# Norm gain rows folded into the row scale of a hybrid decoder block, with the first weight slabs in halves

## The chip, the core and the metric

The kernel runs on one core of a Trainium2 chip. Five engines work side by side and meet through semaphores: TensorE (PE in the profile), VectorE (DVE), ScalarE (ACT), GpSimd (POOL) and SyncE (SP), which here issues every DMA. The metric is device time in microseconds (us) of one launch; lower is better.

## The reference

One decoder block over 512 tokens of width 1024, in float32. What matters here are its two RMS norms, each followed by a projection:

```python
def _rmsnorm(x, g):
    xf = x.astype(jnp.float32)
    xf = xf * lax.rsqrt(jnp.mean(xf * xf, axis=-1, keepdims=True) + EPS)
    return (xf * g.astype(jnp.float32)).astype(x.dtype)

h = _rmsnorm(x, norm_mix[l])
proj = h @ w_in[l]
... two attention branches, merged and gated ...
x = x + merged @ w_out[l]
h2 = _rmsnorm(x, norm_mlp[l])
x = x + jnp.square(jax.nn.relu(h2 @ w_ff1[l])) @ w_ff2[l]
```

Each norm multiplies a token's row by one factor (the row factor) and each of the 1024 columns by a gain (`norm_mix`, `norm_mlp`). Four shorter gains of 64 belong to the norms of the attention heads.

## The kernel before

The program is written out by hand for each engine (`@block.sync`, `gpsimd`, `scalar`, `vector`, `tensor`); each engine runs its list in order, and semaphores are the only ties. Tokens lie in four row blocks of 128 (`m` = 0 to 3), the width in eight chunks of 128. Every large product is made of three matmuls, high x high, high x low and low x high parts, where the high part is the value rounded to float32r (an ACT copy) and the low part the difference (a DVE subtraction): lines 378 to 380 and 385 to 387.

Weights come as slabs of 128 x 2048 (1 MB) into four raw buffers (`load`, line 399). ACT writes a slab's high part (`act_cut`, 340), DVE its low part (`dve_cut`, 365), into one of two cut buffers. Slabs 0 and 1 are the two halves of the depth for the first column group, KVI.

**The first norm.** SP issues x block 0, six small DMAs (both norm gains as 8 x 128, and four head gains), slab 0, x block 1, slab 1, x blocks 2 and 3, and then the rest. For each block ACT squares the rows and sums them (`norm_square`, 548), POOL makes the row factor in two small steps (`rows_rsqrt`, 479), and DVE multiplies the row by it (`norm_scale`, 787). PE turns the block in two halves of four 128 x 128 transposes into PSUM banks 4 and 5 (`norm_turn`, 1085). A half is a unit `u`, two for each block. With tokens now along the columns, the gain is one number for each partition and chunk: DVE multiplies the turned half with it out of PSUM into an SBUF buffer, `rows_t` (`norm_gain`, 791). From `rows_t` ACT makes the high part (`norm_hi`, 551) and DVE the low part (`norm_lo`, 802). The gains themselves were turned by one transpose on PE (line 1106) and copied by ACT (566) into `gain`.

DVE's order is written out at lines 815 to 824: scale of block 0; its two gain multiplies and two low parts; slab 0; scale of block 1; slab 1; then scale of block 2 ahead of the gain and low parts of block 1, scale of block 3 ahead of those of block 2, and those of block 3.

PE begins with 8 filler matmuls (`keep_warm`, 1097: a zero block, result unused), the transpose of the gains, the transposes of block 0 and 27 more fillers. Then it projects block 0 with slab 0, turns block 1, and projects with slab 1; block 1's projection waits for block 1's low parts (`nt_cut`), and so on. `norm_turn` may reuse a PSUM bank as soon as the gain multiply has read it (`nt_gained`).

**The second norm** (lines 737 to 744, 1039 to 1045, 1359 to 1380) runs the same helpers inside the output projection: for each block DVE adds the projection to x (`add_to_x`), scales, and then treats the block before it; PE turns block `m-1` behind block `m`'s projection, and block 3 behind the first part of the first feed-forward product, `ff1_part(0, 0, 256)`.

## Time and profile before

| | |
|---|---|
| Median of 3 runs | 789.45 us (788.76 to 789.53) |
| The profiled execution | 790.06 us |
| Its span, first to last instruction | 788.3 us |
| PE busy | 763.3 us, 97% of the span |
| DVE, ACT, POOL busy | 402.4, 304.9, 132.8 us |
| DMA | 70.11 MB, on average 89 GB/s |

The profile shows one execution. An engine's busy time counts its instructions; PE's are pipelined, so consecutive matmuls start closer together than each one lasts, and their start-to-start distance is what they cost. The chain that ended last is followed back from the last instruction, from each step to what released it. A "record" is one row of PE in the trace: an fp32 product shows as two. The fp32 transposes and the float32r products show as one.

### The profile page before, as it was taken

Reading aid. Unit: us, or ns where it says so; the run is one execution under the profiler, and the core shown is the slowest. Engines: PE = TensorE matmul, PEld = TensorE weight load, DVE = VectorE, ACT = ScalarE, POOL = GpSimd, SP = SyncE. Lnnn points to the kernel's source line nnn. Section 1 sums busy time; section 2 is a strip of 40 time slices with the busy share of each in tenths; the row PEclk is TensorE's granted clock in tenths of the full one; section 3 lists DMA queues with packets and bytes.
Section 4 is the critical chain, followed back from the end, with each engine's and each line's share of the span. In section 5 each row is a group of like instructions: output and inputs, shape, how many; then the busy total and the mean of one; then the engine's idle time right before and its main releaser. Section 6 shows DMA issues by size and latency. Waiting matters only on the chain.

```text
span 788.3 us, 9219 instructions
## 1 busy us (share of the span) xinstructions
PE 763.3 (97%) x3588; PEld 599.2 (76%) x3588; DVE 402.4 (51%) x599; ACT 304.9 (39%) x417; POOL 132.8 (17%) x143
## 2 busy tenths in 40 slices
PE   8999999999997999899999999999999999999998
PEld 4768778777775555588888888888888888888886
DVE  5544887688796856456556433233332233233331
ACT  4325553455554676633323442114311242123310
POOL 3104325000002454003301121002100120002100
PEclk9999999999998999999999999999999999999999
DMA  8307231401011212123090313332233313332011
GB/s 290 145 15 217 103 108 56 131 27 54 16 40 53 54 54 54 54 83 127 5 310 10 107 59 104 105 107 87 74 107 106 106 63 102 102 106 92 15 53 53
DMA packets 47842, 70.11 MB, mean 89 GB/s; under 512 B 2608, under 2 KB 27200, under 8 KB 47808
## 3 DMA queue, kind: packets, MB, share of 16 engines
q1 hardware_dynamic: 47808, 69.65, 27.4%
q8 instruction: 22, 0.36, 0.2%
q14 instruction: 12, 0.10, 0.0%
HBM read 65.19 MB, written 2.10 MB: 85 GB/s over the span
## 4 chain that ended last, share of the span: by engine, by line
PE 87%; DVE 6%; ACT 2%; issue 1%; DMA 1%; POOL 1%; SPq 1%; DVEq 0%; ACTq 0%; POOLq 0%
PE ps L385 13%; PE ps L387 13%; PE ps L386 13%; PE ps L378 13%; PE ps L380 12%; PE ps L379 12%; PE ps L1222 2%; PE ps L1258 2%; PE ps L1299 1%; DVE cut_lo L369 1%; PE ps L1204 1%; PE ps L1289 1%; DMA raw<-in_w_in_dram 1%; PE ps L1234 1%; PE ps L1218 1%
## 5 line engine op out<-in xcount | busy, mean ns | idle before, releaser
L385 PE MATMUL ps<-cut_hi,a_hi 128*128 128x512 f32 x480 | 189.2, 394 | 1.0 <-DVE a_lo L806 1.0
L387 PE MATMUL ps<-cut_hi,a_lo 128*128 128x512 f32 x480 | 187.2, 390 | 0.0
L386 PE MATMUL ps<-cut_lo,a_hi 128*128 128x512 f32 x480 | 187.0, 390 | 0.0
L378 PE MATMUL ps<-b_hi,cut_hi 128*128 128x512 f32 (+1 forms) x336 | 129.8, 386 | 0.5 <-DVE b_lo L806 0.5
L379 PE MATMUL ps<-b_lo,cut_hi 128*128 128x512 f32 (+1 forms) x336 | 129.5, 386 | 0.0
L380 PE MATMUL ps<-b_hi,cut_lo 128*128 128x512 f32 (+1 forms) x336 | 129.5, 386 | 0.0
L369 DVE TENSOR_TENSOR cut_lo<-raw,cut_hi 128x2048 fp32r<-128x2048 f32 (+1 forms) x38 | 78.9, 2079 | 58.9 <-ACT cut_hi L347 58.9
L385 PEld LDWEIGHTS ps<-cut_hi,a_hi 128*128 128x128 f32 x480 | 90.2, 188 | 19.7 <-DVE a_lo L806 1.5
L387 PEld LDWEIGHTS ps<-cut_hi,a_lo 128*128 128x128 f32 x480 | 90.1, 188 | 19.2
L386 PEld LDWEIGHTS ps<-cut_lo,a_hi 128*128 128x128 f32 x480 | 90.2, 188 | 17.5
L362 DVE TENSOR_TENSOR cut_lo<-raw,cut_hi 128x2048 fp32r<-128x2048 f32 x24 | 55.0, 2293 | 83.5 <-ACT cut_hi L356 83.5
L347 ACT ACTIVATE cut_hi<-raw 128x2048 fp32r<-128x2048 f32 (+1 forms) x38 | 65.5, 1726 | 63.2 <-PE ps L387 38.3
L540 POOL TENSOR_TENSOR a_lo<-gates,a_hi 128x512 fp32r<-128x512 f32 x32 | 41.5, 1297 | 273.2 <-ACT a_hi L751 273.2
L356 ACT ACTIVATE cut_hi<-raw 128x2048 fp32r<-128x2048 f32 x24 | 45.8, 1909 | 101.9 <-PE ps L387 101.9
L378 PEld LDWEIGHTS ps<-b_hi,cut_hi 128*128 128x128 f32 x336 | 63.4, 189 | 14.5 <-DVE b_lo L806 0.7
L380 PEld LDWEIGHTS ps<-b_hi,cut_lo 128*128 128x128 f32 x336 | 63.4, 189 | 14.0
L379 PEld LDWEIGHTS ps<-b_lo,cut_hi 128*128 128x128 f32 x336 | 63.4, 189 | 13.9
L1052 DVE SCALAR_TENSOR_TENSOR gates<-ps,gates 128x512 f32<-128x512 f32 x32 | 22.1, 692 | 84.2 <-ACT gates L749 82.6
L378 PE MATMUL ps<-a_hi,cut_hi 128*128 128x512 f32 x128 | 55.4, 433 | 3.3 <-ACT gates L665 3.3
L1030 DVE TENSOR_TENSOR gates<-ps,gates 128x512 f32<-128x512 f32 x40 | 27.6, 690 | 54.5 <-PE ps L387 54.4
L749 ACT ACTIVATE gates<-ps 128x512 f32<-128x512 f32 x32 | 19.2, 599 | 90.3 <-PE ps L380 90.3
L529 POOL TENSOR_SCALAR qo_sb<-qo_sb 128x128 f32<-128x128 f32 (+3 forms) x28 | 30.2, 1080 | 132.7 <-DVE snmax L973 132.0
(136 smaller groups left out, 897.2 us busy)
## 6 DMA issues: line engine op xcount, KB each, us to landing
raw<-in_w_ff_dram SPq DMA_DIRECT2D x32, 1024.0 KB, 5.4
raw<-in_w_in_dram SPq DMA_DIRECT2D x18, 1024.0 KB, 5.2
gates<-in_x_dram SPq DMA_DIRECT2D x8, 512.0 KB, 4.9
raw<-in_w_out_dram SPq DMA_DIRECT2D x4, 1024.0 KB, 5.0
raw<-in_w_branch_sb_dram SPq DMA_DIRECT2D x2, 1024.0 KB, 5.1
raw<-in_w_branch_sa_dram SPq DMA_DIRECT2D x4, 512.0 KB, 6.2
out_dram<-gates SPq DMA_DIRECT2D x8, 256.0 KB, 2.0
gates<-sp_hi SPq DMA_DIRECT2D x8, 128.0 KB, 2.4
```

Source lines behind the costliest of these rows:

```text
L347: cut = nc.scalar.activation(cut_slot(i, cut_hi, part, parts), raw[:, i % RAW, part * w:(part + 1) * w], ACT.Copy)
L356: nc.scalar.activation(cut_slot(i, cut_hi, 0, 1), raw[:, i % RAW, :], ACT.Copy).then_inc(hi_done, 1)
L362: nc.vector.tensor_tensor(cut_slot(i, cut_lo, 0, 1), raw[:, i % RAW, :], cut_slot(i, cut_hi, 0, 1).bitcast(F32), ALU.subtract).then_inc(lo ...
L369: cut = nc.vector.tensor_tensor(cut_slot(i, cut_lo, part, parts), raw[:, i % RAW, part * w:(part + 1) * w], cut_slot(i, cut_hi, part, part ...
L378: nc.tensor.matmul(dst, w_hi, rhs_hi, start=start, stop=False)
L379: nc.tensor.matmul(dst, w_hi, rhs_lo, start=False, stop=False)
L380: return nc.tensor.matmul(dst, w_lo, rhs_hi, start=False, stop=stop)
L385: nc.tensor.matmul(dst, l_hi, w_hi, start=start, stop=False)
L386: nc.tensor.matmul(dst, l_hi, w_lo, start=False, stop=False)
L387: return nc.tensor.matmul(dst, l_lo, w_hi, start=False, stop=stop)
L529: pool.tensor_scalar(bias, sa_bias[(n - 1) % 4][:, 0:w], 2.0 ** (sa_head(n - 1) - sa_head(n)), None, ALU.mult).then_inc(bias_done, 1)
L540: pool.tensor_tensor(a_lo[:, c, :], ff_sq[c % 2], a_hi[:, c, :].bitcast(F32), ALU.subtract).then_inc(f1_cut, 1)
```

## The change

1. **Gain with the row factor.** `norm_scale` becomes one DVE instruction, (x times row factor) times gain row, over 1024 columns. `norm_gain` and `rows_t` go; `norm_hi` and `norm_lo` read the turned half in PSUM directly, and `norm_turn` waits for the low part (`nt_cut`) before it reuses a bank.
2. **Where the gain rows come from.** `norm_mix` comes as one row of 1024; PE multiplies a row of ones with it (two fp32 matmuls of 512 columns, depth 1), which spreads it over all partitions in banks 6 and 7. It stays there until block 3 is scaled. `norm_mlp` comes by a DMA that repeats its row on all partitions, issued ahead of x block 2 of the second norm.
3. **The head gains** are loaded behind the x blocks, and turned behind block 2's projection; ACT copies and scales them after block 3's high parts.
4. **Halves.** Slabs 0 and 1 are each loaded, cut and waited for in two halves of 128 x 1024. The first block's projection runs in four quarters of 6 matmuls, each behind its own wait, and block 1 is turned behind the third quarter.
5. **Filler.** 27 matmuls become 7, and write to bank 3.

```diff
-WARM = (8, 27)
+WARM = (8, 7)
...
+            def load_half(i, hf):
+                dst = raw[:, i, :].rearrange("p (k c) -> p k c", k=4)
+                sp.dma_start(dst[:, 2 * hf:2 * hf + 2, :], rows(win, 512 * i + 256 * hf, 2, GROUPS[KVI], 512)
+                             ).then_inc(raw_in[i] if hf else half_in[i], 16)
+
+            load_half(0, 0)
+            sp.dma_start(mix_row, norm_mix).then_inc(mix_row_in, 16)
+            load_half(0, 1)
             sp.dma_start(x_tok[:, 1, :], x_d[P:2 * P, :]).then_inc(x_in[1], 16)
-            load(1)
+            load_half(1, 0)
+            load_half(1, 1)
...
                 sp.wait_ge(mg_cut, 4 * (m // 2) + 4)
+                if m == 2:
+                    sp.dma_start(mlp_gain, norm_mlp.to_broadcast([P, D])).then_inc(mlp_gain_in, 16)
...
             pool.memset(minus_half[:, :], -0.5)
+            pool.memset(one_row, 1.0).then_inc(one_row_made, 1)
...
-                act.wait_ge(nt_gained, u + 1)
+                act.wait_ge(nt_done, u + 1)
                 A(dst[:, 4 * hf:4 * hf + 4, m * P:(m + 1) * P],
-                  rows_t(u).rearrange("p (a b) -> p a b", a=4), ACT.Copy).then_inc(nt_hi, 1)
+                  bank(4 + u % 2).rearrange("p (a b) -> p a b", a=4), ACT.Copy).then_inc(nt_hi, 1)
...
-                V.tensor_scalar(dst, src, row_r[:, m:m + 1], None, ALU.mult).then_inc(row_scaled, 1)
+                V.scalar_tensor_tensor(out=dst, in0=src, scalar=row_r[:, m:m + 1], in1=g,
+                                       op0=ALU.mult, op1=ALU.mult).then_inc(row_scaled, 1)
...
+            mix_gain = ps[:, 6 * S:8 * S]
+            dve.wait_ge(mix_spread, 1)
+            norm_scale(0, x_tok[:, 0, :], x_tok[:, 0, :], mix_gain)
+            dve_half(0)
+            norm_lo(0, a_hi, a_lo)
+            dve_cut(0, 1, 2)
+            norm_lo(1, a_hi, a_lo)
+            dve_half(1)
+            norm_scale(1, x_tok[:, 1, :], x_tok[:, 1, :], mix_gain)
+            dve_cut(1, 1, 2)
             for m in range(2, TB):
-                norm_scale(m, x_tok[:, m, :], x_tok[:, m, :])
-                norm_block(m - 1, 0, a_hi, a_lo)
-            norm_block(3, 0, a_hi, a_lo)
+                norm_scale(m, x_tok[:, m, :], x_tok[:, m, :], mix_gain)
+                norm_lo(2 * m - 2, a_hi, a_lo)
+                norm_lo(2 * m - 1, a_hi, a_lo)
...
                     if u >= 2:
-                        pe.wait_ge(nt_gained, u - 1)
+                        pe.wait_ge(nt_cut, u - 1)
...
-            pe.wait_ge(gains_in, 96)
-            T.transpose(bank(7, 0, 20), gain_rows[:, :], ident[0:20, 0:20]).then_inc(gain_t, 1)
+            pe.wait_ge(one_row_made, 1)
+            pe.wait_ge(mix_row_in, 16)
+            for hf in range(2):
+                mm = T.matmul(bank(6 + hf), one_row, mix_row[:, hf * S:(hf + 1) * S], start=True, stop=True)
+            mm.then_inc(mix_spread, 1)
...
+                    if first and k == 0:
+                        pe.wait_ge(half_cut, half + 1)
+                        pe.wait_ge(nt_cut, half + 1)
+                    if first and k == 2:
+                        if half:
+                            norm_turn(1, x_tok[:, 1, :])
+                        slab_ready(half)
```

DVE's list at the start of the program, before (`cut_lo` is a slab's low part, `a_lo` that of the turned x, `gates` the buffer that holds x and `rows_t`):

```order
L789 TENSOR_SCALAR gates<-gates,row_r 128x1024
L797 TENSOR_TENSOR gates<-ps,gain 128x512 x2
L806 TENSOR_TENSOR a_lo<-gates,a_hi 128x4x128 x2
L369 TENSOR_TENSOR cut_lo<-raw,cut_hi 128x2048
L789 TENSOR_SCALAR gates<-gates,row_r 128x1024
L369 TENSOR_TENSOR cut_lo<-raw,cut_hi 128x2048
L789 TENSOR_SCALAR gates<-gates,row_r 128x1024
L797 TENSOR_TENSOR gates<-ps,gain 128x512 x2
L806 TENSOR_TENSOR a_lo<-gates,a_hi 128x4x128 x2
```

And now, up to block 1's low parts:

```order
L813 SCALAR_TENSOR_TENSOR gates<-gates,row_r,ps 128x1024 [waits row_ready,mix_spread]
L825 TENSOR_TENSOR cut_lo<-raw,cut_hi 128x1024 [waits half_hi]
L820 TENSOR_TENSOR a_lo<-ps,a_hi 128x4x128 [waits nt_hi]
L375 TENSOR_TENSOR cut_lo<-raw,cut_hi 128x1024 [waits hi_done]
L820 TENSOR_TENSOR a_lo<-ps,a_hi 128x4x128 [waits nt_hi]
L825 TENSOR_TENSOR cut_lo<-raw,cut_hi 128x1024 [waits half_hi]
L813 SCALAR_TENSOR_TENSOR gates<-gates,row_r,ps 128x1024 [waits row_ready]
L375 TENSOR_TENSOR cut_lo<-raw,cut_hi 128x1024 [waits hi_done]
L813 SCALAR_TENSOR_TENSOR gates<-gates,row_r,ps 128x1024 [waits row_ready]
L820 TENSOR_TENSOR a_lo<-ps,a_hi 128x4x128 [waits nt_hi] x2
```

The gain multiplies (L797) are gone, the slabs' low parts are cut in two and stand between block 0's steps, and the first scale has a second wait.

PE's list at the start, before:

```order
L1100 MATMUL ps<-cold_b,const_b 128x512 [waits const_cut]
L1100 MATMUL ps<-cold_b,const_b 128x512 x7
L1106 MATMUL ps<-ident,lg 128x20 [waits gains_in,ident_done]
L1093 MATMUL ps<-ident,gates 128x128 [waits row_scaled]
L1093 MATMUL ps<-ident,gates 128x128 x7
L1100 MATMUL ps<-cold_b,const_b 128x512 x27
L385 MATMUL ps<-cut_hi,a_hi 128x512 [waits lo_done,nt_cut]
```

And now:

```order
L1122 MATMUL ps<-cold_b,const_b 128x512 [waits const_cut]
L1122 MATMUL ps<-cold_b,const_b 128x512 x7
L1130 MATMUL ps<-lg,dist 128x512 [waits mix_row_in,one_row_made,ident_done]
L1130 MATMUL ps<-lg,dist 128x512
L1115 MATMUL ps<-ident,gates 128x128 [waits row_scaled]
L1115 MATMUL ps<-ident,gates 128x128 x7
L1122 MATMUL ps<-cold_b,const_b 128x512 x7
L391 MATMUL ps<-cut_hi,a_hi 128x512 [waits nt_cut,half_cut]
```

The two matmuls that spread the gain row (L1130) stand between the first fillers and the transposes of block 0, in place of the gains' transpose.

DVE's list in the second norm, before, from the last slab ahead of it (`b_lo` is the low part of the second norm's output):

```order
L369 TENSOR_TENSOR cut_lo<-raw,cut_hi 128x2048 [waits hi_done] x2
L1030 TENSOR_TENSOR gates<-ps,gates 128x512 [waits wo_done]
L789 TENSOR_SCALAR gates<-gates,row_r 128x1024 [waits row_ready]
L1030 TENSOR_TENSOR gates<-ps,gates 128x512 [waits wo_done]
L789 TENSOR_SCALAR gates<-gates,row_r 128x1024 [waits row_ready]
L797 TENSOR_TENSOR gates<-ps,gain 128x512 [waits nt_cut,nt_done] x2
L806 TENSOR_TENSOR b_lo<-gates,b_hi 128x4x128 [waits nt_hi] x2
```

And now:

```order
L375 TENSOR_TENSOR cut_lo<-raw,cut_hi 128x2048 [waits hi_done] x2
L1049 TENSOR_TENSOR gates<-ps,gates 128x512 [waits wo_done]
L813 SCALAR_TENSOR_TENSOR gates<-gates,row_r 128x1024 [waits row_ready,mlp_gain_in]
L1049 TENSOR_TENSOR gates<-ps,gates 128x512 [waits wo_done]
L813 SCALAR_TENSOR_TENSOR gates<-gates,row_r 128x1024 [waits row_ready]
L820 TENSOR_TENSOR b_lo<-ps,b_hi 128x4x128 [waits nt_hi] x2
```

Each block loses its two gain multiplies; its scale has a gain row as second tensor.

## Rows read from the trace of the kernel before

**Rows 1.** The page's section 4, the chain that ended last, by engine.

```profile
PE 87%; DVE 6%; ACT 2%; issue 1%; DMA 1%; POOL 1%; SPq 1%; DVEq 0%; ACTq 0%; POOLq 0%
```

**Rows 2.** Waits of 0 to 62 us: who waited for whom, sum, times, longest.

```profile
PE ps L385 <- DVE a_lo L806: 1.0, 1, 1.0
```

**Rows 3.** PE's timeline, 0 to 16: start, duration, line, output and inputs, count, [idle before].

```profile
3.56 3.60 PE L1100 MATMUL ps<-cold_b,const_b 128*128 128x512 bf16 x8 [3.56 <-DVE const_b L785]
...
7.31 1.97 PE L1093 MATMUL ps<-ident,gates 128*128 128x128 f32 x8
9.08 6.11 PE L1100 MATMUL ps<-cold_b,const_b 128*128 128x512 bf16 x27
14.95 0.47 PE L385 MATMUL ps<-cut_hi,a_hi 128*128 128x512 f32 x1
```

**Rows 4.** The chain that ended last, around 22: start, time on it, engine and line.

```profile
21.25 1.30 DVE a_lo L806 x2
...
23.10 0.23 PE ps L386
```

**Rows 5.** Windows: length, busy PE, PEld, DVE, ACT, POOL, clock share, DMA share, GB/s.

```profile
9.08:14.95 5.87, 5.87 (x29) 2.63 (x27) 4.43 (x5) 5.43 (x6) 1.26 (x2) 1.00 1.04 404
22.60:52.00 29.40, 29.40 (x138) 22.63 (x139) 13.89 (x27) 8.51 (x17) 4.32 (x10) 1.00 0.19 67
```

**Rows 6.** The chain near 171: the fp32 matmuls of 128 columns at line 1218.

```profile
170.83 0.44 PE ps L1218 x4
```

**Rows 7.** Timeline of DVE and PE in the first norm.

```profile
12.51 2.29 DVE L369 TENSOR_TENSOR cut_lo<-raw,cut_hi 128x2048 fp32r<-128x2048 f32 x1 [1.11 <-ACT cut_hi L347]
...
25.47 1.04 PE L1093 MATMUL ps<-ident,gates 128*128 128x128 f32 x8
...
26.11 0.69 DVE L797 TENSOR_TENSOR gates<-ps,gain 128x512 f32<-128x512 f32 x1 [1.55 <-PE ps L1093]
```

**Rows 8.** Groups by line and shape, whole span: count, busy us, mean ns, idle before.

```profile
L949 DVE SCALAR_TENSOR_TENSOR lg<-ps,lg 128x1280 f32<-128x1280 f32 x8 | 11.9, 1492 | 11.9 <-ACT lg L661 11.6
...
L369 DVE TENSOR_TENSOR cut_lo<-raw,cut_hi 128x1024 fp32r<-128x1024 f32 x8 | 9.8, 1219 | 3.0 <-ACT cut_hi L347 3.0
...
L749 ACT ACTIVATE gates<-ps 128x512 f32<-128x512 f32 x32 | 19.2, 599 | 90.3 <-PE ps L380 90.3
...
L549 ACT ACTIVATE gates<-gates 128x1024 f32<-128x1024 f32 x8 | 8.4, 1053 | 13.1 <-DVE gates L1030 11.1 <-DMA gates<-in_x_dram 2.0
L347 ACT ACTIVATE cut_hi<-raw 128x1024 fp32r<-128x1024 f32 x8 | 8.4, 1048 | 0.0
```

**Rows 9.** POOL's row factor: one instance, and both steps (ns: least/median/most).

```profile
13.60 1.25 POOL L482 TENSOR_SCALAR row_ms<-row_ss 128x1 f32<-128x1 f32 x1 [7.44 <-ACT gates L549]
...
L482 POOL TENSOR_SCALAR row_ms<-row_ss x8: 192/193/1871, 5.3 to 429.5; 128x1 f32<-128x1 f32 x8
...
L483 POOL TENSOR_TENSOR row_r<-row_ms,minus_half x8: 550/554/577, 5.6 to 429.7; 128x1 f32<-128x1 f32 x8
```

**Rows 10.** Timeline of DVE and PE in the second norm.

```profile
400.09 0.69 DVE L1030 TENSOR_TENSOR gates<-ps,gates 128x512 f32<-128x512 f32 x1 [2.03 <-PE ps L387]
...
414.56 1.09 PE L1093 MATMUL ps<-ident,gates 128*128 128x128 f32 x8 [0.97 <-DVE gates L789]
...
430.34 0.75 DVE L789 TENSOR_SCALAR gates<-gates,row_r 128x1024 f32<-128x1024 f32 x1 [2.13 <-POOL row_r L483]
...
431.84 1.16 PE L1093 MATMUL ps<-ident,gates 128*128 128x128 f32 x8 [0.62 <-DVE gates L797]
...
436.33 0.39 PE L378 MATMUL ps<-b_hi,cut_hi 128*128 128x256 f32 x1 [0.47 <-DVE b_lo L806]
```

**Rows 11.** PE's longest stop: windows (clock share third from last), and the work after it.

```profile
245.00:245.50 0.50, 0.00 (x0) 0.00 (x0) 0.47 (x3) 0.00 (x0) 0.00 (x0) 0.50 0.00 0
251.50:252.00 0.50, 0.50 (x3) 0.36 (x3) 0.47 (x5) 0.07 (x1) 0.47 (x1) 0.85 0.00 0
...
246.74 0.45 PE L1289 MATMUL ps<-ident,lg 128*128 128x128 f32 x1 [4.63 <-DVE lg L1003]
```

More of the change, by code:

```diff
@@ L108, in block_kernel @@
         dist_i = dist[:, :].bitcast(I32)
-        gain = sb("gain", [P, 20], F32)
+        gain = sb("gain", [P, 4], F32)
         w_tok = sb("w_tok", [P, TB, IXH], F32)
@@ L186, in block_kernel @@
         x2_in = [sem(f"x2_in{j}") for j in range(TB)]
+        mix_row_in = sem("mix_row_in")
+        one_row_made = sem("one_row_made")
+        mix_spread = sem("mix_spread")
+        mlp_gain_in = sem("mlp_gain_in")
         gains_in = sem("gains_in")
+        half_in = [sem(f"half_in{j}") for j in range(2)]
+        half_hi = sem("half_hi")
+        half_cut = sem("half_cut")
         kw_in = sem("kw_in")
@@ L208, in block_kernel @@
         nt_done = sem("nt_done")
-        nt_gained = sem("nt_gained")
         nt_hi = sem("nt_hi")
@@ L564, in _ @@
                 if m == 0:
-                    act.wait_ge(gain_t, 1)
-                    A(gain[:, :], bank(7, 0, 20), ACT.Copy).then_inc(gain_ready, 1)
+                    act_half(0)
                     norm_hi(0, a_hi)
                     norm_hi(1, a_hi)
-                    act_cut(0)
+                    act.wait_ge(raw_in[0], 16)
+                    act_cut(0, 1, 2)
                 elif m == 1:
-                    act_cut(1)
+                    act_half(1)
+                    act.wait_ge(raw_in[1], 16)
+                    act_cut(1, 1, 2)
                 else:
@@ L576, in _ @@
             norm_hi(7, a_hi)
-            for j in (16, 18):
+            act.wait_ge(gain_t, 1)
+            A(gain[:, :], bank(7, 0, 4), ACT.Copy).then_inc(gain_ready, 1)
+            act.wait_ge(gain_ready, 1)
+            for j in (0, 2):
                 A(gain[:, j:j + 1], gain[:, j:j + 1], ACT.Copy, scale=HD ** -0.5).then_inc(gain_ready, 1)
@@ L596, in turned @@
                 if g == KVI:
-                    A(k_sa[:, t], bank(b, 0, P), ACT.Copy, scale=gain[:, 19:20])
+                    A(k_sa[:, t], bank(b, 0, P), ACT.Copy, scale=gain[:, 3:4])
                     A(q_parts[0][:, :, t], bank(b, P, 3 * P).rearrange("p (a b) -> p a b", a=2),
@@ L1099, in keep_warm @@
                 for _ in range(n):
-                    T.matmul(bank(6), ident_b, cold_b[:, :], start=True, stop=True)
+                    T.matmul(bank(3), ident_b, cold_b[:, :], start=True, stop=True)
             pe.wait_ge(const_cut, 1)
@@ L1148, in _ @@
             keep_warm(WARM[1])
-            for m in range(TB):
+            project_part(KVI, 0, 0, first=True)
+            project_part(KVI, 1, 0, first=True).then_inc(proj_done, 1)
+            for m in range(1, TB):
                 pe.wait_ge(nt_cut, 2 * m + 2)
-                if m == 0:
-                    slab_ready(0)
                 project_part(KVI, 0, m)
-                if m == 0:
-                    norm_turn(1, x_tok[:, 1, :])
-                    slab_ready(1)
                 if m == 1:
```

63 lines of the change are left out of this document (28 added, 35 removed).

## The prediction, made before the changed kernel ran

> **What bounds the kernel now.** I read the page first: TensorE (PE) carries 87% of the chain that ended last [rows 1]. So only time in which PE stands still, or works at filler, can be won. Next, who waits: in the start PE waits once, 1.0 us, for the low part of row block 1 [rows 2]. Third, PE's own timeline [rows 3]: 3.56 us idle, 8 filler matmuls, the transposes of row block 0, 27 fillers, the first projection at 14.95. Fourth, the chain ahead of row block 1's projection, which DVE's low parts end at 22.55 [rows 4], and the stretch behind it, in which PE has no gap until 52 [rows 5]. **Whatever moves the start of block 1's projection, 22.60, moves the end; an earlier 14.95 alone moves nothing.** What the reader should see: DVE and the small steps on POOL own that chain, not the transfers.
>
> **Filler and transfers.** Twenty of 35 filler matmuls go; they filled a wait and are worth nothing by themselves. Six small DMAs ahead of the first slab go to later or out, and slabs 0 and 1 come in halves. x block 0 and slab 0 are 1.57 MB, 3.9 us at 404 GB/s [rows 5]; issued from 0.8 on they land near 6 or 7, while the steps below first want the second half at 13.0. Earlier transfers are hidden, with 6 us of cover. The head gains and the k/w columns are wanted behind four row blocks of some 24 matmuls at 0.23 [rows 4], 5.5 us each, so after 40: nothing.
>
> **When the gain row is in PSUM.** This is the new wait: DVE's first scale waits for mix_spread, which PE makes behind 8 fillers, and the chain of block 0 and then of block 1 is queued behind that scale. A filler takes 0.43 (8 last until 7.1 [rows 3]), which is 512 columns at 1.2 GHz; a memset on POOL adds 0.1, so the spread starts near 7.15. It is two fp32 matmuls of 512 columns with a depth of one row, which the trace has not. Nearest is an fp32 product of 128 columns, two records each, 4 records in 0.44 [rows 6]: 0.11 a record, so 0.44 at 512 columns, 1.76 for the spread's 4 at 2.4 GHz and 3.5 at 1.2. Which level holds? The transposes start 0.22 apart (8 from 7.31 to 9.08), twice what 128 fp32 columns take later, and the 27 fillers are done by 15, 0.22 each, which is 2.4 GHz [rows 3]. So the clock rose near 9.1, and I take the same here: 1.95 us at the low level do 56%, the rest needs 0.75, the end is 9.85 and DVE starts at **10.0**. Bounds: 9.1 (high throughout), 10.8 (low throughout). Before, PE already transposed at 7.31; this wait eats the head start that shorter steps give.
>
> **The DVE chain from 10.0.** Scale and gain in one pass over 1024 columns has no row; 0.69 at 512 columns [rows 7] and 1.492 at 1280 [rows 8] put it at 1.23, where the plain scale takes 0.75 [rows 10]. A low part takes 0.69, half a slab 1.22 on DVE and 1.05 on ACT, a high part out of PSUM 0.60, a square 1.05 [rows 8] and 0.19 for its sum. Neighbours on DVE overlap by some 0.09 (a pair of low parts lasts 1.30 [rows 4]). Then:
> - DVE: scale to 11.2. PE: transposes 11.25 to 12.15; the first four are seen 0.65 after their start (25.47, 26.11 [rows 7]), at 11.9. ACT: high parts to 13.05, second half of slab 0 to 14.05. DVE: its low part to 15.3, low part of block 0 to 15.9.
> - ACT: square of block 1 to 15.15, first half of slab 1 to 16.2. DVE: its low part to 17.4, scale of block 1 to 18.55, last half slab to 19.7.
> - PE: 7 fillers to 13.7, the quarters of block 0 to 15.1, 16.7, 18.8, transposes of block 1 to 19.7, last quarter to 21.1: in time.
>
> The gain multiplies are gone, two of 0.69 for each block, but the scale is 0.47 dearer, halves repeat a fixed part, and DVE idles from 13.2 to 14.05 for ACT. Block 2's scale stands ahead of block 1's low parts on DVE, so its row factor counts. ACT squares until 18.3. POOL's first step takes 0.19, but up to 1.87 when DVE was in a cut, as the one from 13.60 that ends with DVE's cut of 12.51 at 14.85 [rows 7, 9]; the second takes 0.55 [rows 9]. The last half slab's cut runs from 18.5 to 19.7, so I take the factor at 20.25, the scale to 21.4, two low parts to 22.65. Block 1 starts at **22.7, 0.1 later than 22.60**. Should POOL slip past the cut, it is 0.5 earlier.
>
> The Trainium skill (SBUF — State Buffer, "SBUF: two separate sides") says that DVE and GpSimd hold a shared port pair by an exclusive lock, also when a DVE instruction with two SBUF inputs meets a GpSimd one that reads SBUF. By that rule the cut locks POOL out and the new scale, with its gain in PSUM, doesn't; the row at 13.60 agrees. By it the sum has the 0.1 later, without it the 0.5 earlier.
>
> **The second norm.** The gain row comes by one more DMA of 0.5 MB, 1.3 us at 404 GB/s, ahead of x blocks 2 and 3. DVE adds block 2 at 400.09 [rows 10], some 6 us after SP issues it: hidden; the price is 1.3 if that cover were gone. The scale grows by 0.47, and PE waits for it at 414.56 [rows 10]: all behind is 0.47 later. In the last block the scale, 430.34 before, ends at 432.05. PE's transposes now wait for the low parts of block 2 (nt_cut in place of nt_gained), which DVE does behind that scale: 432.65 for the first four, 433.25 for the others, where before they started at 431.84. They end at 433.7, 24 narrow matmuls at half of 0.23 and a little end at 436.65, and the last low part (435.2) is no longer late; before, this point was 436.33 [rows 10]. **Cost 0.3 us**, bounds 0 (the last stop and its 0.47 end as before) and 0.8 (both delays add).
>
> The Trainium skill (VectorE: DVE Perf Modes, "The perf-mode tier table") speaks against the change: a one-tensor fp32 pass in SBUF runs at double rate, a two-tensor pass or one on PSUM does not. The rows agree. At the double rate the scale would stay at 0.75, and the second norm would win 0.6 instead, since the old waits of 0.62 and 0.47 would go.
>
> **Sum.** 0.1 + 0.3 = 0.4 us later. Against the profiled execution, 790.06 us (span 788.3, 1.8 around it), that is 790.5; against the median of the three runs, 789.45, it is **789.9**. 0.2% is 1.6 us, about what a measurement of this kernel can tell from no change.
>
> **Rivals.**
> First, *the early spread*: the clock rises before the spread, and POOL slips past the cut. DVE starts at 9.1 and block 1 12.05 later, at 21.15: 1.45 won, 0.3 lost, 788.3. For it: one trace shows the clock's rise once. Against: its transposes from 7.31 were slow.
> Second, *slower: the clock falls*. 27 fillers kept PE busy; now PE stands still from 9.85 to 11.25 for the new wait on DVE, and between quarters. At the low level 7 fillers take 3.0 instead of 1.5, transposes 1.8 instead of 0.9, a quarter 2.6 instead of 1.4. The trace shows this once: PE stops 4.63 us before 246.74, the granted clock is 0.50 at 245, and it rises again near 251.6, after 4.9 us of work [rows 11]. With 4.9 us low from 11.25, the quarters start at 16.2, block 1's transposes end at 21.4 and its low parts at 24.0: 1.3 more, 791.2. Low until block 1 starts: about 3 more, 792.9. It decides from the point where the quarters start later than 14.9. Against: 1.4 us of stop is nearer to the 1.0 ahead of 22.60, behind which matmuls start 0.23 apart [rows 2, 4], than to the 3 us that brought 0.50.
> Third, *more than I see*: halves let blocks overlap so well that over 1.6 us come off, 787.5. Block 1's projection would have to start before 20.7, though DVE has 10.4 us of work ahead of it; so the first scale would need to start before 10.0 and DVE never idle.
> Fourth, *nothing reaches PE*: block 1 starts as before and the second norm costs nothing, 789.4; it lies in the forecast's own range.
>
> **How the numbers follow.** Forecast with its bounds and the fourth (789.0 to 790.9): 0.56. Early spread, or one of its two parts (788.0 to 789.0): 0.20. Clock falls (mostly 791.0 to 792.9): 0.16. More than I see: 0.08. The range leaves out the third and the worse half of the second: 788.0 to 791.6. Faster by over 0.2% means under 787.9: 0.08. Slower by over 0.2% means over 791.0: 0.15. Within: 0.77.
>
> **What would show it.** DVE's first scale at 10.0 and 1.23 long; four records of the spread, the last shorter than the first; block 1's projection at 22 to 23; POOL's steps for block 2 drawn out to the end of the last half cut; the scale near 413.7 at 1.23, and the work behind it 0.3 to 0.5 late. I am wrong if the first scale starts before 9, if block 0's projection matmuls stand 0.43 apart, or if PE waits between 23 and 400 where it did not.

## The result, and the profile after

The changed kernel takes 792.17 us (median of 22 runs, 789.16 to 792.72), the kernel before, timed beside it, 789.13 (22 runs, 788.50 to 789.87). The ratio is 1.0027, with a 95% interval of 1.0021 to 1.0034. So the change costs 2.1 us by the ratio and 3.0 by the medians. A second set of 11 runs gave 1.0017 (1.0006 to 1.0028). The two measures differ because the times of the changed kernel fall into three groups. In the 33 runs of both sets they are 788.9 to 789.5 (6 runs), 790.2 to 790.8 (11) and 792.1 to 792.7 (16). The kernel before has two groups that lie closer together: in its 80 runs beside the experiments below, 788.3 to 789.2 (46 runs) and 789.2 to 790.2 (34). They are told apart by the mean granted clock of a run, the share of full speed that the profile records for TensorE: 0.997 or 0.998 in the first group, 0.995 or 0.996 in the second. The profiled execution of before, 790.06 at 0.995, is of the second. The forecast was 789.9, within 0.2% of before. What came is slower by 0.27% in the first set and by 0.17% in the second.

The profiled execution belongs to the last group: 792.67 us, with a span of 791.0 against 788.3. The page first: PE still carries the chain, 89% of it where it was 87% [rows 1].

```profile
span 791.0 us, 9166 instructions
...
PE 763.6 (97%) x3572; PEld 598.5 (76%) x3572; DVE 396.5 (50%) x585; ACT 303.6 (38%) x419; POOL 131.1 (17%) x144
...
PE 89%; DVE 6%; ACT 3%; issue 1%; POOL 1%; DVEq 0%; POOLq 0%; ACTq 0%
```

DVE has 5.9 us less work and ACT 1.3 less, and that brought nothing. PE's timeline in the start, the columns as in [rows 3]:

```profile
3.69 3.60 PE L1122 MATMUL ps<-cold_b,const_b 128*128 128x512 bf16 x8 [3.69 <-DVE const_b L809]
7.21 3.78 PE L1130 MATMUL ps<-lg,dist 1*128 1x512 f32 x4
12.37 1.97 PE L1115 MATMUL ps<-ident,gates 128*128 128x128 f32 x8 [1.38 <-DVE gates L813]
14.13 2.73 PE L1122 MATMUL ps<-cold_b,const_b 128*128 128x512 bf16 x7
16.51 0.58 PE L391 MATMUL ps<-cut_hi,a_hi 128*128 128x512 f32 x1
...
24.46 0.50 PE L391 MATMUL ps<-cut_hi,a_hi 128*128 128x512 f32 x1 [1.22 <-DVE a_lo L820]
```

L1130 is the spread, four records in 3.78 us. L1115 are transposes (L1093 before), L391 is the first product of each projection triple. The reader should see that everything up to about 15.9 runs at 1.2 GHz: the eight transposes take 1.76 to the next start, 0.22 each, and the seven fillers take 2.38, where they would take 3.0 at the low level and 1.5 at the high one. (The 15.9 is an estimate: 1.75 us at the low level and 0.63 at the high one make seven fillers in 2.38.) Before the change, the same engine had reached 2.4 GHz near 9.1 [rows 3]. Block 1's projection, which sets the end, starts at 24.46 instead of 22.60 [rows 4, 5]. DVE and POOL in the same stretch:

```profile
11.03 1.28 DVE L813 SCALAR_TENSOR_TENSOR gates<-gates,row_r,ps 128x1024 f32<-128x1024 f32 x1 [7.40 <-PE ps L1130]
...
20.27 1.22 DVE L375 TENSOR_TENSOR cut_lo<-raw,cut_hi 128x1024 fp32r<-128x1024 f32 x1
21.93 1.28 DVE L813 SCALAR_TENSOR_TENSOR gates<-gates,row_r,ps 128x1024 f32<-128x1024 f32 x1 [0.44 <-POOL row_r L498]
23.13 1.28 DVE L820 TENSOR_TENSOR a_lo<-ps,a_hi 128x512 fp32r<-128x512 f32 x2
```

```profile
20.24 1.65 POOL L498 TENSOR_TENSOR row_r<-row_ms,minus_half 128x1 f32<-128x1 f32 x1
```

DVE stands still for 7.40 us ahead of its first scale, for the spread. POOL's second step for block 2 takes 1.65 instead of 0.55. It ends at 21.89, 0.40 behind the end of DVE's last half cut, which ran from 20.27 to 21.49.

Two more places lose time. The transpose of the head gains (L1193) now stands between two projections on PE, and L1197 is the first product behind the four blocks (L1165 before, at 40.88):

```profile
37.07 0.39 PE L393 MATMUL ps<-cut_hi,a_lo 128*128 128x512 f32 x1
37.39 0.22 PE L1193 MATMUL ps<-ident,lg 4*128 4x4 f32 x1
37.54 0.50 PE L391 MATMUL ps<-cut_hi,a_hi 128*128 128x512 f32 x1
37.87 0.40 PE L392 MATMUL ps<-cut_lo,a_hi 128*128 128x512 f32 x1
...
43.11 0.40 PE L1197 MATMUL ps<-a_hi,sp_hi 128*40 128x512 f32 x1
```

From block 1's first product to this one (24.46 to 43.11) it is 18.65 now and was 18.28 (22.60 to 40.88). In the second norm both of PE's waits grew, from 0.97 to 1.58 and from 0.62 to 1.13 [rows 10]:

```profile
417.90 1.09 PE L1115 MATMUL ps<-ident,gates 128*128 128x128 f32 x8 [1.58 <-DVE gates L813]
...
435.71 1.16 PE L1115 MATMUL ps<-ident,gates 128*128 128x128 f32 x8 [1.13 <-DVE b_lo L820]
```

From DVE's add for block 1 (413.64, before 410.90) to its first work behind the norm (443.29, before 440.14) it is 29.65 and was 29.24. The sum of the three: 1.86 + 0.37 + 0.41 = 2.64, of the 2.7 by which the span grew. That they add up so well is in part luck, since other stretches changed too and cancel. Behind PE's long stop near 245 it is 10.94 to PE's next wait and was 10.41, for the clock is low there (see the section on the changed kernel again). From 443.29 to the end it is 347.7 and was 348.2 (from 440.14), though nothing was changed there; no run says why.

### The profile page after: what moved, and what is told of

The parts are those of the page before. It is cut to its first block, busy times and chain, and to the rows that moved or that the text cites. A ratio compares the mean times of both kernels' runs of the same rounds, so it can differ in the third digit from the quotient of the medians.

```text
span 791.0 us, 9166 instructions
## 1 busy us (share of the span) xinstructions
PE 763.6 (97%) x3572; PEld 598.5 (76%) x3572; DVE 396.5 (50%) x585; ACT 303.6 (38%) x419; POOL 131.1 (17%) x144
## 4 chain that ended last, share of the span: by engine, by line
PE 89%; DVE 6%; ACT 3%; issue 1%; POOL 1%; DVEq 0%; POOLq 0%; ACTq 0%
PE ps L391 13%; PE ps L392 13%; PE ps L393 13%; PE ps L384 13%; PE ps L386 12%; PE ps L385 12%; PE ps L1254 2%; PE ps L1290 2%; PE ps L1331 1%; DVE cut_lo L375 1%; PE ps L1236 1%; PE ps L1321 1%; PE ps L1266 1%; PE ps L1115 1%; PE ps L1250 1%
## 5 line engine op out<-in xcount | busy, mean ns | idle before, releaser
L391 PE MATMUL ps<-cut_hi,a_hi 128*128 128x512 f32 x480 | 189.5, 395 | 1.2 <-DVE a_lo L820 1.2
L391 PEld LDWEIGHTS ps<-cut_hi,a_hi 128*128 128x128 f32 x480 | 90.1, 188 | 19.9 <-DVE a_lo L820 1.6
L375 DVE TENSOR_TENSOR cut_lo<-raw,cut_hi 128x2048 fp32r<-128x2048 f32 (+1 forms) x38 | 76.8, 2022 | 55.3 <-ACT cut_hi L353 55.3
L353 ACT ACTIVATE cut_hi<-raw 128x2048 fp32r<-128x2048 f32 (+1 forms) x38 | 63.8, 1681 | 59.4 <-PE ps L393 34.8
```

The costliest lines, as they stand in the source:

```text
L353: cut = nc.scalar.activation(cut_slot(i, cut_hi, part, parts), raw[:, i % RAW, part * w:(part + 1) * w], ACT.Copy)
L375: cut = nc.vector.tensor_tensor(cut_slot(i, cut_lo, part, parts), raw[:, i % RAW, part * w:(part + 1) * w], cut_slot(i, cut_hi, part, part ...
L391: nc.tensor.matmul(dst, l_hi, w_hi, start=start, stop=False)
```

## The experiments

Two theories stood against each other. **A**: the new wait for the spread makes the loss, since the spread runs at the low clock and DVE's whole chain is queued behind it. **B**: the halves, the order of DVE's chain and the dearer second norm make it. All kernels below ran in three batches beside the kernel before, which had medians of 788.89, 788.74 and 789.46. The ratios are each against the kernel before in the same batch; the last column is read from one trace of each kernel.

| kernel | median us | ratio (95%) | block 1 starts |
|---|---|---|---|
| spread ahead of the fillers | 791.59 | 1.0029 (1.0018 to 1.0041) | 23.65 |
| gain row by repeating DMA | 787.35 | 0.9979 (0.9970 to 0.9988) | 19.78 |
| spread with depth 128 | 789.46 | 1.0000 (0.9991 to 1.0009) | 22.36 |
| second norm as before | 790.49 | 1.0019 (1.0010 to 1.0028) | 22.50 |
| head gains turned early | 790.35 | 1.0026 (1.0017 to 1.0036) | 22.42 |
| before, with one-row fillers | 796.10 | 1.0090 (1.0076 to 1.0103) | 29.48 |
| DMA, whole slabs | 789.80 | 1.0010 (1.0001 to 1.0019) | 22.95 |
| combined: DMA, old second norm, gains early | 786.63 | 0.9969 (0.9957 to 0.9981) | 19.96 |
| changed kernel again | 790.71 | 1.0017 (1.0006 to 1.0028) | 24.45 |
| combined, low parts first | 785.55 | 0.9951 (0.9938 to 0.9964) | 19.22 |
| changed, low parts first | 789.53 | 1.0003 (0.9993 to 1.0014) | 21.58 |
| before, with the halves alone | 788.93 | 0.9989 (0.9980 to 0.9997) | 20.77 |

### The gain row without a spread

```diff
+            sp.dma_start(mlp_gain, norm_mix.to_broadcast([P, D])).then_inc(mix_row_in, 16)
...
-            sp.dma_start(mix_row, norm_mix).then_inc(mix_row_in, 16)
...
-            mix_gain = ps[:, 6 * S:8 * S]
-            dve.wait_ge(mix_spread, 1)
+            mix_gain = mlp_gain
+            dve.wait_ge(mix_row_in, 16)
...
-                mm = T.matmul(bank(6 + hf), one_row, mix_row[:, hf * S:(hf + 1) * S], start=True, stop=True)
```

> No spread: the gain row comes repeated on all partitions by one DMA of 0.5 MB behind x block 0, the scale reads it from SBUF. Theory A: the first scale starts as early as its row factor allows, near 7; transposes near 8.3; block 1's first projection about 4 us earlier than 24.46, at 20.5 to 21.5, so 3 to 4 us less than the changed kernel and 0 to 1 us less than the kernel before (the second norm's 0.45 and the head gains' 0.34 stay). Theory B: block 1 starts no earlier than 22.6, as POOL's row factors, locked out by DVE's cuts, and ACT's share of the halves own the chain; at most 1.9 us less.

It took 787.35: 1.5 us less than before. Relative to before that is 4.6 us less than the changed kernel by the medians, and 3.8 by the ratios (0.9979 against 1.0027). PE, DVE and POOL of this kernel:

```profile
7.96 1.06 PE L1114 MATMUL ps<-ident,gates 128*128 128x128 f32 x8 [0.95 <-DVE gates L812]
...
19.78 0.50 PE L391 MATMUL ps<-cut_hi,a_hi 128*128 128x512 f32 x1 [1.55 <-DVE a_lo L819]
```

```profile
6.53 1.28 DVE L812 SCALAR_TENSOR_TENSOR gates<-gates,row_r 128x1024 f32<-128x1024 f32 x1 [3.03 <-DMA gates<-in_norm_mix_dram]
...
17.25 1.28 DVE L812 SCALAR_TENSOR_TENSOR gates<-gates,row_r 128x1024 f32<-128x1024 f32 x1 [0.72 <-POOL row_r L497]
```

The first scale starts 4.5 us earlier and block 1 4.7 us earlier. Theory B's limit (no earlier than 22.6) is broken, and theory A's own figure (20.5 to 21.5) was too late. The DMA moves 0.5 MB where the row alone is 4 KB, and it is the cheaper way: it lands at 6.5, when the row factor of block 0 has just come (6.26).

### The spread's place

```diff
-            pe.wait_ge(const_cut, 1)
-            keep_warm(WARM[0])
-            pe.wait_ge(ident_done, 1)
             pe.wait_ge(one_row_made, 1)
             pe.wait_ge(mix_row_in, 16)
...
             mm.then_inc(mix_spread, 1)
+            pe.wait_ge(const_cut, 1)
+            keep_warm(WARM[0])
+            pe.wait_ge(ident_done, 1)
```

> The two spread matmuls stand ahead of the 8 fillers on PE, nothing else. Theory A (the place of the spread and the low clock level make the loss): the spread runs from 3.7 to 7.4, DVE's first scale starts near 7.5 instead of 11.03, PE's 8 fillers run behind the spread and end near 10.9 at the low level, so the transposes start near 10.9 instead of 12.37 and block 1's first projection moves from 24.46 to about 23.0: 1.5 us less than the changed kernel. Theory B (the halves, the order of DVE's chain and the dearer second norm make it): block 1's projection stays within 0.4 of 24.46, and the time within 0.5 us of the changed kernel's.

```profile
5.37 3.75 PE L1127 MATMUL ps<-lg,dist 1*128 1x512 f32 x4 [5.37 <-DMA lg<-in_norm_mix_dram]
...
12.43 1.04 PE L1115 MATMUL ps<-ident,gates 128*128 128x128 f32 x8
```

The spread did not start at 3.7, since its row lands only at 5.37. So the scale came at 9.15, the eight fillers held the transposes back until 12.43, and block 1 started at 23.65: 0.8 earlier than in the changed kernel, not 1.5. The expectation was wrong in its first number, and the time (ratio 1.0029) shows no gain. Part of the reason is what it is compared with: about half of the changed kernel's runs are in the two lower groups. Six of the seven runs here lie at 791.4 to 791.9, about 0.7 below the changed kernel's upper group, and the seventh, the traced one, at 790.56. The row teaches something else: the transposes last 1.04 and so stand at 2.4 GHz. PE had done 3.75 us of one-row matmuls, all at 1.2 GHz, and then 3.4 us of full ones.

### The spread's depth

```diff
-        one_row = dist[0:1, 0:P]
+        one_row = dist[:, 0:P]
...
+            V.memset(lg[:, 1, 0:D], 0.0).then_inc(mix_zero, 1)
...
-                mm = T.matmul(bank(6 + hf), one_row, mix_row[:, hf * S:(hf + 1) * S], start=True, stop=True)
+                mm = T.matmul(bank(6 + hf), one_row, lg[:, 1, hf * S:(hf + 1) * S], start=True, stop=True)
```

> The spread stays behind the 8 fillers but has a depth of 128 rows (127 of them zero) instead of one; DVE clears the block ahead of the DMA, which costs about 0.5 us where nothing waits. Theory A in its strong form (a matmul of one row is no work to the clock): the granted clock rises near 9.1 as before the change, the spread's later records take half of 0.93, the first scale starts at 10.0 instead of 11.03, the transposes stand 0.11 to 0.15 apart and block 0's fillers 0.22, and block 1 starts near 23.2: 1.2 us less than the changed kernel's longer executions. Weak form (only the order on PE counts) and theory B: the spread's four records stay at 0.93 each and the first scale at 11.0, time as the changed kernel's within 0.3.

```profile
7.09 2.63 PE L1133 MATMUL ps<-lg,dist 128*128 128x512 f32 x4
11.09 1.09 PE L1118 MATMUL ps<-ident,gates 128*128 128x128 f32 x8 [1.37 <-DVE gates L816]
```

The strong form of theory A came out: a spread of 2.63 instead of 3.78, the scale at 9.76 instead of 11.03 (10.0 had been expected), transposes at 2.4 GHz. Block 1 started at 22.36, 0.8 earlier than expected. The same columns on the same engine with 127 added rows of zeros give 0.27% back, the whole loss, and no run of 11 was over 789.9.

### One-row fillers in the kernel before

```diff
-                    T.matmul(bank(6), ident_b, cold_b[:, :], start=True, stop=True)
+                    T.matmul(bank(6), ident_b[0:1, :], cold_b[0:1, :], start=True, stop=True)
```

> The kernel before the change, but its 35 fillers have a depth of one row instead of 128 (same 512 columns, same place). If matmuls of one row are no work to the clock: the granted clock does not rise near 9.1, the 27 fillers stand 0.43 apart and last until about 20.7 instead of 15, block 0's first projection moves from 14.95 to about 20.7, block 1's from 22.60 to 28 or later, and the time is 5 to 7 us longer than before. If the low clock of the changed kernel's start came of its waits and its order alone: the fillers stand 0.22 apart from 9.1 as before, block 1 starts at 22.6, and the time is that of the kernel before within 0.5.

```profile
9.01 11.70 PE L1100 MATMUL ps<-cold_b,const_b 1*128 1x512 bf16 x27
20.63 0.80 PE L385 MATMUL ps<-cut_hi,a_hi 128*128 128x512 f32 x1
...
25.49 0.51 PE L387 MATMUL ps<-cut_hi,a_lo 128*128 128x512 f32 x1
25.84 1.04 PE L1093 MATMUL ps<-ident,gates 128*128 128x128 f32 x8
```

This is the plainest row of the case. PE is busy without a gap from 3.55 on, the 27 fillers stand 0.43 apart until 20.6, and 2.4 GHz comes only near 25.5, 4.9 us after block 0's projection began. Block 1 starts at 29.48. It costs 7.4 us (5 to 7 had been expected). The waits play no part here, since the instructions and their order are those of the kernel before.

### Whole slabs, and the halves alone

The first is the kernel with the repeating DMA, with slabs 0 and 1 loaded, cut and projected in one piece. The second is the kernel before with nothing but the halves and 7 fillers instead of 27 behind the transposes.

```diff
-            load_half(0, 0)
...
-            load_half(0, 1)
+            load(0)
...
-            dve_half(0)
             norm_lo(0, a_hi, a_lo)
-            dve_cut(0, 1, 2)
             norm_lo(1, a_hi, a_lo)
-            dve_half(1)
+            dve_cut(0)
```

> As the kernel with the repeating DMA (787.35, block 1 at 19.78), but slabs 0 and 1 whole as before the change: loaded, cut and projected in one piece. If the halves carry part of the gain: ACT's and DVE's cuts of slab 0 (2.1 and 2.3) delay block 1's square and scale, and block 1 starts at 20.9, 1.1 later, 788.4 in all. If they carry nothing (the gain is all from the scale with the gain in it): within 0.3 of 787.35.

> The kernel before the change with the halves alone (loads, cuts and quarters of slabs 0 and 1, and 7 fillers instead of 27); the gain is multiplied behind the transposes as before, no spread. If the halves carry the gain: block 1 starts near 20.3 instead of 22.60, and the time is 786.6 to 787.0, 2 us less than before. If halves and the gain in the scale need each other (ACT's head start is then no use): block 1 at 22 or later, within 0.6 of before.

Whole slabs cost 2.4 us, not 1.1 (by the medians and by the ratios, against the kernel with the repeating DMA). The first row below is from the kernel with whole slabs, and behind it stand two of its windows (length, busy PE, clock share, DMA share, GB/s); the last fence is from the kernel before with the halves alone.

```profile
14.88 0.47 PE L391 MATMUL ps<-cut_hi,a_hi 128*128 128x512 f32 x1 [2.33 <-DVE cut_lo L375]
```

```profile
16.00:18.00 2.00, 2.00 (x7) 0.50 1.03 361
18.00:20.00 2.00, 2.00 (x12) 0.79 1.06 388
```

```profile
20.77 0.50 PE L388 MATMUL ps<-cut_hi,a_hi 128*128 128x512 f32 x1 [1.95 <-DVE a_lo L824]
21.11 0.48 PE L389 MATMUL ps<-cut_lo,a_hi 128*128 128x512 f32 x1
21.38 0.63 PE L390 MATMUL ps<-cut_hi,a_lo 128*128 128x512 f32 x1
```

With whole slabs PE stands still for 2.33 us, and then the granted clock is 0.50 from about 15.4 to 18.8. DVE's low parts of block 1 are done at 21.9, but PE itself is late and starts block 1 at 22.95. With the halves alone block 1 starts at 20.77, 1.8 earlier than before (20.3 had been expected), but after a stop of 1.95 the granted clock is 0.50 from 21.3 to 24.7, and 1.6 us of it are lost again: from block 1's first product to the first one behind the four blocks it is 19.86 (to 40.63) and was 18.28. The median is 788.93. So the halves are worth 2.4 us where the gain is in the scale, and 0.5 (by the medians) to 0.9 (by the ratio) where it is not. That small gain is a mixture. The traced run has a mean clock of 0.996, and seven of the 12 runs, with 0.996 or less, lie at 788.8 to 789.4. The five others have 0.997 or 0.998 and lie at 787.0 to 788.0 (middle one 787.26), where before's runs of that mean clock in the same batch have a median of 788.87. No trace shows one of the five, but 0.998 leaves no room for a fall in the start beside the one near 245, so the halves alone seem to be worth 1.6 where the clock holds. The scale with the gain in it, but with whole slabs, is worth nothing: 1.0010, in which the second norm and the head gains have their 0.8 us.

### The second norm and the head gains

The second norm gets its old form back; then, apart from that, the head gains' transpose goes from behind block 2 to the wait ahead of block 1.

```diff
...
-                    norm_scale(TB + m, xn2[m % 2], xres[:, m, :], mlp_gain)
+                    plain_scale(TB + m, xn2[m % 2], xres[:, m, :])
                 if m >= 1:
+                    norm_gain(2 * (TB + m) - 2)
+                    norm_gain(2 * (TB + m) - 1)
```

> The first norm as changed, the second norm in its old form (plain scale, gain multiplies ahead of the cuts, head gains' transpose with 12 rows). Both theories: DVE's scale ahead of 417.90 is 0.75 instead of 1.28, the wait there falls from 1.58 to 0.97, the last turn's from 1.13 to 0.62. Theory A: that is worth 0.4 us of the changed kernel's loss and no more, block 1 stays at 24.46. Theory B (the second norm carries the loss through its DMA and its waits): 1.5 us or more.

```diff
+            pe.wait_ge(gains_in, 64)
+            T.transpose(bank(3, 0, 4), gain_rows[:, :], ident[0:4, 0:4]).then_inc(gain_t, 1)
             for m in range(1, TB):
...
-                if m == 2:
-                    pe.wait_ge(gains_in, 64)
-                    T.transpose(bank(7, 0, 4), gain_rows[:, :], ident[0:4, 0:4]).then_inc(gain_t, 1)
```

> The head gains' transpose stands ahead of block 1's projection, in a wait that PE has anyway (1.22 in the changed kernel), instead of between blocks 2 and 3. If the missed term is right, the stretch from block 1's first projection to the first transposes of its result loses 0.34 (18.65 to about 18.3) and the time 0.3 us; block 1's own start stays (24.46, or 22.5 where the clock rises early). Rival: the transpose costs nothing where it stood, and the time stays within 0.1; or ACT's copy of the gains, wanted now by block 3, holds PE up.

With the old second norm the waits are 0.97 and 0.62 again and the stretch of 29.65 is 29.24: 0.41. With the gains turned early the stretch of 18.65 is 18.27: 0.38. The times agree (ratios 1.0019 and 1.0026 against 1.0027), but for the second the effect is smaller than the interval, and only its trace shows it. In the kernel with the old second norm there is also less time behind the norm, 347.4 from DVE's first work there to the end, where it was 347.7 in the changed kernel; so its whole gain is not the second norm's.

Both traces show more. PE in the kernel with the gains early, then windows of it (length, busy PE, clock share, DMA share, GB/s):

```profile
6.98 1.98 PE L1130 MATMUL ps<-lg,dist 1*128 1x512 f32 x4
10.33 1.97 PE L1115 MATMUL ps<-ident,gates 128*128 128x128 f32 x8 [1.38 <-DVE gates L813]
```

```profile
9.00:11.00 2.00, 0.67 (x3) 0.77 1.04 396
11.00:13.00 2.00, 2.00 (x10) 0.50 1.04 425
13.00:15.00 2.00, 2.00 (x10) 0.87 1.12 302
```

Here the clock rose before the spread: its four records take 1.98 instead of 3.78, and the scale starts at 8.99. But the granted clock fell to 0.50 near 10.2, at the end of the stop of 1.38 behind the spread, and stayed there until about 13.5. Block 1 starts at 22.42, 2.0 earlier than in the changed kernel's trace.

### The changed kernel again

> The changed kernel once more. If its two groups of times (789.2 to 790.8, 792.1 to 792.7) are the two levels of the clock in the spread, then a trace with a span of 789.0 or less has a spread of 1.98 to 2.2, its first scale near 9.1 and block 1 near 22.5, and a trace with a span of 790.5 or more has 3.78, 11.0 and 24.5. If the groups have another cause, the span does not go with the spread's length.

The trace has a span of 790.9, a spread of 3.78, the scale at 11.02 and block 1 at 24.45. That fits, but it is the same group once more, so the short spread is shown only by kernels that differ in one place elsewhere. The mean granted clock of every run supports the reading for the middle group: it is 0.993 or 0.994 in each of its runs, as in the trace just shown with its fall (0.993), and 0.995 or 0.996 in every other run.

What sets the two lower groups apart can be something else, far behind the change. In every trace PE stands still for 4.6 us near 245, waiting for DVE, and around the end of that stop the clock falls. Here are the stop and PE's next wait in the changed kernel, and in the changed kernel with DVE's order turned (the last experiment below):

```profile
249.09 0.44 PE L1321 MATMUL ps<-ident,lg 128*128 128x128 f32 x1 [4.64 <-DVE lg L1022]
...
260.03 0.47 PE L384 MATMUL ps<-a_hi,cut_hi 128*128 128x512 f32 x1 [0.61 <-ACT gates L689]
```

```profile
246.48 0.42 PE L1321 MATMUL ps<-ident,lg 128*128 128x128 f32 x1 [4.64 <-DVE lg L1022]
...
256.25 0.47 PE L384 MATMUL ps<-a_hi,cut_hi 128*128 128x512 f32 x1 [0.62 <-ACT gates L689]
```

The stretch of 240 to 260 shows how long the fall lasts. The columns are those of [rows 5]. First the changed kernel (before and with the gains early the share is 0.83 too), then the one with DVE's order turned (with the deep spread it is 0.91 too):

```profile
240.00:260.00 20.00, 14.79 (x67) 9.73 (x63) 13.94 (x42) 8.87 (x24) 5.41 (x8) 0.83 0.15 51
```

```profile
240.00:260.00 20.00, 14.74 (x72) 9.96 (x68) 13.81 (x44) 10.74 (x33) 6.04 (x8) 0.91 0.13 34
```

A share of 0.83 is about 6.8 us at half rate, 0.91 about 3.5. What that is worth shows in the time from the end of the stop to PE's next wait: 10.9 in both traces of the changed kernel and 10.8 with the gains early, but 9.7 to 9.8 in the five traces with the short fall. That is 1.1 to 1.2 us, about what lies between the groups at 789 and 790.5 (their medians are 1.3 apart). In the other traces with the long fall, that of the kernel before among them, more of it lies inside the stop, and it is 10.1 to 10.7. The trace with DVE's order turned has both, a fall in the start (0.83 over 10 to 20) and the short one near 245, and its run has a time of 788.86 and a mean clock of 0.996, like the runs of the group at 789. So that group can have the same start as the middle one. No trace of the changed kernel itself shows it.

### The terms together, and DVE's order

```diff
-                norm_scale(m, x_tok[:, m, :], x_tok[:, m, :], mix_gain)
                 norm_lo(2 * m - 2, a_hi, a_lo)
                 norm_lo(2 * m - 1, a_hi, a_lo)
+                norm_scale(m, x_tok[:, m, :], x_tok[:, m, :], mix_gain)
```

The first kernel has the repeating DMA, the old second norm and the early head gains. The second adds the order above to it, the third puts that order into the changed kernel.

> Gain row by the repeating DMA (no spread), the second norm in its old form, and the transpose of head gains (12 rows) in the wait ahead of block 1. If the terms add: 787.35 of the kernel with the repeating DMA, less 0.45 for the second norm and 0.34 for the transpose, is 786.6, which is 2.3 us less than before. If they do not add (PE waits for something else in the second norm, or ACT's copy of the gains is late for block 3): 787.0 or more.

> The combined kernel (786.63, block 1 at 19.96), with DVE making the two low parts of block m-1 ahead of the scale of block m instead of behind it. If that scale and its wait for POOL's row factor (0.72) own the end of the chain: the low parts end near 18.4, PE's wait of 1.41 ahead of block 1 falls to about 0.1, and the time falls by 1.2 to 1.4, to 785.3. If the high parts of ACT or PE itself are as late as the scale was: under 0.3 won. Against it: block 2's transposes then wait for its scale; they are wanted 2.8 after block 1 starts, near 21.3, and the scale ends near 19.7.

> The changed kernel with only that order turned (low parts of block m-1 ahead of the scale of block m). If the dearer scale and the POOL step that is locked out by the last half cut are on the path: block 1 starts 1.0 to 1.3 earlier than in the changed kernel, at 23.2 with the long spread or at 21.3 with the short one, and the median falls by 1.0 to 1.3 us. If the path runs through PE's transposes and ACT's high parts: block 1 within 0.3 of 24.46 or 22.5.

The terms add: 786.63 came for 786.6, closer than the traces bear out, since in this kernel too the work behind the second norm takes less than in the changed one (351.2 from the end of PE's last wait in the norm, 433.72, to the end; in the kernel before it is 352.0, from 436.33). The order is worth 1.1 us more by the medians and 1.4 by the ratios: 785.55, ratio 0.9951, the best version, 3.9 us below before. Its PE and DVE:

```profile
18.97 0.23 PE L1198 MATMUL ps<-ident,lg 12*128 12x12 f32 x1
19.22 0.50 PE L396 MATMUL ps<-cut_hi,a_hi 128*128 128x512 f32 x1
```

```profile
17.88 1.29 DVE L837 TENSOR_TENSOR a_lo<-ps,a_hi 128x512 fp32r<-128x512 f32 x2 [0.75 <-ACT a_hi L573]
19.09 1.27 DVE L816 SCALAR_TENSOR_TENSOR gates<-gates,row_r 128x1024 f32<-128x1024 f32 x1
```

The wait ahead of block 1 (1.41) is gone, and PE runs without a stop from 12.32 on. In the changed kernel the same order cuts the way from the first scale to block 1 from 13.43 to 12.19 (9.39 to 21.58), and the median by 1.2 us (789.53 for 790.71, in the same batch). POOL's locked-out step is still there (1.65 at 18.41) and no longer matters, since the low parts go first.

## What the prediction had right and what it had wrong, point by point

- **What bounds, and where it shows: right, but for a second place.** Block 1's projection, with the two fixed terms, gives the change of the span for the changed kernel (2.64 of 2.7), with some luck. In the traces with the short fall near 245 the span is shorter than this sum by 1.0 to 1.3 more: with the spread ahead of the fillers it gives 790.1 (788.3 + 1.05 + 0.78), and the span was 788.8. The prediction had that fall in view [rows 11] and did not ask whether it lasts as long in every run.
- **When the gain row is in PSUM: the step that failed.** It said "So the clock rose near 9.1, and I take the same here". The four records and their price (1.76 at 2.4 GHz, 3.5 at 1.2; measured 1.98 and 3.78) were close, but the rise was read off one trace as if it belonged to the program, and one-row work was taken to bring the clock up as full-depth fillers did. With the one-row spread it came before the spread, at its very start, or not at all during it: the scale starts at 9.0 to 9.4 or at 11.0. Only where the depth was restored did it start between (9.76). The upper bound of 10.8 was 0.2 short.
- **The chain behind it: right at 2.4 GHz, low at 1.2.** From scale to block 1 I had 12.7. With a deep spread it is 12.60. With transposes and fillers at the low level it is 13.43, in both groups that traces show. So the forecast of 22.7 is missed by 1.03 in the spread and by 0.73 in the chain. A scale of 1.28 for 1.23 is a small part of it.
- **The lock between DVE and POOL: right.** POOL's step was drawn out past the end of the last half cut, 1.65 for 0.55, in the changed kernel and in five variants. The Trainium skill (SBUF — State Buffer, "SBUF: two separate sides") has an exclusive lock between the two engines for this case. The trace agrees: POOL's step started with the cut (20.24 and 20.27) and ended at 21.89, when the cut had ended at 21.49. What I did not see is that the low parts need not stand behind that scale at all.
- **The second norm: 0.41 for 0.3.** Both of PE's waits grew, by 0.61 and 0.51, about the 0.53 by which the scale is dearer; the last wait of 0.47 went, as foretold. The scale takes 1.28. The Trainium skill (VectorE: DVE Perf Modes, "The perf-mode tier table") has it that `tensor_tensor` in fp32 does not run at the double rate; the scale, which also reads two tensors, agrees with it (1.28 for 0.75).
- **The head gains: missed.** "After 40: nothing" was said of their DMAs. Their transpose stands between two projections that PE would run without a gap and costs 0.37.
- **The rivals.** The second gave the right size (791.2 to 792.9) at 0.16. Its mechanism, a fall of the clock behind the new stop, is real (0.50 from 10.5 on in two traces, and behind 11 in a third), but the largest group of runs has another one: the clock had not risen yet. I held 1.4 us of stop to be near to the 1.0 of [rows 2]; what stood ahead of the stop, a spread of one row, was left out of the comparison. With a deep spread the same stop of 1.37 brought no fall in the trace. The first rival, the early spread, came in part: three traces show the scale at 9.0 to 9.4. But its chain of 12.05 was 13.43 in two of them, since the clock fell and POOL did not slip past the cut, and its 788.3 lacks the head gains too.
- **The range**, 788.0 to 791.6, ends 0.6 below the median of 792.17. By the ratio, on the 789.45 that the forecast started from, the result is 791.6, just the end of the range. The direction was right and the size was not: 0.4 us were forecast, and 2.1 to 3.0 came.

What stays open: no trace of the changed kernel shows its two lower groups; that they have the early rise, and differ by the length of the fall near 245, is read from kernels that differ in one place and from the mean clocks. And why half of the executions see the rise early and half do not is not settled by any run, nor why the fall near 245 has two lengths. The kernel with the repeating DMA and its variants show both too: with full-depth fillers from 3.55 on and one stop of 0.9, the transposes at 8.0 took 1.06 in two traces and 1.94 in two others.

## What to carry to other kernels

Price a wait in the start of a kernel at both clock levels; a rise that one trace shows at one time is no property of the program. Before times that differ by a us are compared, look for the other places where the clock differs from run to run, here one that was 220 us away. Filler, and work that stands in for filler, should use the full depth of rows. A broadcast over partitions by a repeating DMA can be cheaper than one on PE, if the load lies beside other work and the matmul would lie on the chain. And before a dearer instruction is accepted on a chain, see whether the chain's consumer needs it at all: here it could go behind the low parts.

## What the runs showed of the hardware

- One-row matmuls keep PE busy and do not bring the clock up: with fillers of one row (and 1.9 us of transposes among them), 17 us of gapless work stayed at 1.2 GHz, and 2.4 GHz came 4.9 us after full-depth products began, near 25.5. With full-depth fillers and no one-row work it came between 7 and 12.
- The granted clock in the profile reads 1.00 in that whole stretch (and in the changed kernel up to 15.9), though matmuls of 512 columns stand 0.43 apart. Before the first rise, only the distance of the matmuls tells the level; after it, a fall does show (0.50).
- A stop of 1.38 behind one-row work brought 0.50, as did stops of 1.95 (with 1.57 some 9 us ahead of it), 2.33 and 4.6; stops of 0.95, 1.37, 1.55 and 1.58 behind full-depth work did not, in the traces taken. Around the same stop of 4.6 the low clock lasted 3.5 us or 6.8.
- An fp32 matmul of 512 columns and one row gives two records and costs 1.0 us at 2.4 GHz and 1.9 at 1.2. A small depth makes it no cheaper: with 128 rows a record lasts 1.06 at 1.2 GHz and 0.59 at 2.4, and with one row the same.
- DVE's scale with a gain row takes 1.28 for 1024 columns with the gain in PSUM or in SBUF alike.
